# Layer 0's down product by one level of Strassen's scheme, in a fused two-layer diffusion backbone on one core

## The reference

```python
D_FF = (8 * D_MODEL // 3) // 128 * 128        # 2688 = 21 chunks of 128
def conv_ffn(h, w_up, conv_w, conv_b, w_down):
    u = h @ w_up
    ...                                        # convolution over tokens, per channel
    a, b = jnp.split(u, 2, axis=-1)
    return (jax.nn.gelu(a) * b) @ w_down       # (768 x 2688) @ (2688 x 1024) in layer 0
def post_add(x, y, g, gate):
    return x + gate * rms_norm(y, g)           # follows it; y is the product
```

## Time and profile before

| | |
|---|---|
| median of 3 runs | 1529.39 us (1529.23 to 1532.17) |
| profiled execution, first to last instruction | 1530.5 us; no other time is recorded for it |
| instructions | 21741 |
| mean granted TensorE clock | 0.985 of full speed |
| busy: TensorE, VectorE, ScalarE, GpSimd | 1458.3, 966.0, 697.7, 585.9 us |

### The profile page before, as it was taken

One profiled execution on the slowest core, in us unless ns is written; L12 is line 12 of the kernel. 1 busy time (PEld: TensorE's weight loads), 2 busy tenths in 40 slices (PEclk: granted clock), 3 DMA queues, 4 the chain that ended last, 5 costly groups with the idle time before them and its releaser, 6 DMA issues.

```text
span 1530.5 us, 21741 instructions
## 1 busy us (share of the span) xinstructions
PE 1458.3 (95%) x7604; PEld 1192.9 (78%) x7604; DVE 966.0 (63%) x1463; ACT 697.7 (46%) x1184; POOL 585.9 (38%) x516
## 2 busy tenths in 40 slices
PE   4989899999999999999999899899999999999998
PEld 1877567778888888887888688677778888888886
DVE  2368787568678667833346578798876544446445
ACT  3323676444333233223354445588774544444222
POOL 2331545333322222223335522475543444444443
PEclk8999999999999999999999899899999999999999
DMA  8230840223455345411122122010003233333331
GB/s 352 62 97 3 303 175 19 84 97 116 128 156 170 112 126 170 123 63 55 57 70 79 55 75 74 28 42 1 1 9 89 84 97 97 97 98 112 99 97 72
DMA packets 126154, 147.06 MB, mean 96 GB/s; under 512 B 6964, under 2 KB 95288, under 8 KB 125056
## 3 DMA queue, kind: packets, MB, share of 16 engines
q1 hardware_dynamic: 125440, 145.81, 30.1%
q10 hardware_dynamic: 640, 0.26, 0.1%
HBM read 143.92 MB, written 2.14 MB: 95 GB/s over the span
## 4 chain that ended last, share of the span: by engine, by line
PE 86%; DVE 5%; ACT 3%; DMA 2%; issue 2%; POOL 1%; SPq 0%; POOLq 0%; DVEq 0%; ACTq 0%
PE ps L515 24%; PE ps L516 24%; PE ps L517 23%; PE ps L1522 4%; PE ps L1508 4%; PE ps L1533 2%; PE ps L1535 2%; DMA start_w<-in_ada_w_dram 2%; PE ps L1416 1%; PE ps L1010 1%; ACT prob L1564 1%; PE ps L882 1%; DMA ada_w<-in_ada_w_dram 1%; POOL prob L1694 0%; ACT pT_hi L1579 0%
## 5 line engine op out<-in xcount | busy, mean ns | idle before, releaser
L507 POOL TENSOR_TENSOR w_lo<-raw,w_hi 128x1024 fp32r<-128x1024 f32 (+1 forms) x158 | 335.1, 2124 | 586.9 <-ACT w_hi L501 586.9
L515 PE MATMUL ps<-hT_hi,w_hi 128*128 128x512 f32 (+1 forms) x1096 | 387.4, 354 | 4.4 <-DVE hT_lo L1988 3.7
L516 PE MATMUL ps<-hT_lo,w_hi 128*128 128x512 f32 (+1 forms) x1096 | 385.0, 351 | 0.0
L517 PE MATMUL ps<-hT_hi,w_lo 128*128 128x512 f32 (+1 forms) x1096 | 382.7, 349 | 0.0
L501 ACT ACTIVATE w_hi<-raw 128x1024 fp32r<-128x1024 f32 (+1 forms) x179 | 168.8, 944 | 182.6 <-PE ps L517 159.8
L515 PEld LDWEIGHTS ps<-hT_hi,w_hi 128*128 128x128 f32 x1096 | 207.3, 189 | 41.6 <-DVE hT_lo L1988 5.6
L517 PEld LDWEIGHTS ps<-hT_hi,w_lo 128*128 128x128 f32 x1096 | 206.5, 188 | 28.8
L516 PEld LDWEIGHTS ps<-hT_lo,w_hi 128*128 128x128 f32 x1096 | 207.2, 189 | 26.6
L2448 DVE TENSOR_TENSOR g_lo<-act_g,g_hi 128x768 fp32r<-128x768 f32 (+1 forms) x55 | 86.1, 1571 | 126.2 <-ACT g_hi L2398 125.9
L515 PE MATMUL ps<-w_hi,g_hi 128*128 128x512 f32 x380 | 148.2, 390 | 0.8 <-DVE g_lo L2448 0.5
L517 PE MATMUL ps<-w_hi,g_lo 128*128 128x512 f32 x380 | 148.0, 390 | 0.0
(11 more groups left out here) (267 smaller groups left out, 2458.1 us busy)
## 6 DMA issues: line engine op xcount, KB each, us to landing
raw<-in_ffn_w_up_dram SPq DMA_DIRECT2D x84, 512.0 KB, 3.9
ada_w_up<-in_ada_w_dram SPq DMA_DIRECT2D x48, 512.0 KB, 4.2
ada_w<-in_ada_w_dram SPq DMA_DIRECT2D x32, 512.0 KB, 4.8
raw<-in_ffn_w_down_dram SPq DMA_DIRECT2D x42, 256.0 KB, 2.6
raw<-in_ffn_w_down_dram SPq DMA_DIRECT2D x21, 512.0 KB, 3.5
start_w<-in_ada_w_dram SPq DMA_DIRECT2D x8, 1024.0 KB, 8.5
raw<-in_c_w_qkv_dram SPq DMA_DIRECT2D x12, 512.0 KB, 3.7
raw<-in_ab_w_in_dram SPq DMA_DIRECT2D x8, 512.0 KB, 4.1
```

The source lines that it names most:

```text
L507: by.tensor_tensor(split_to(w_lo, phase, m, width), split_from(phase, m, width), split_to(w_hi, phase, m, width).bitcast(F32), ALU.subtrac ...
L515: nc.tensor.matmul(outp, s_hi, m_hi, start=first, stop=False, skip_group_check=True)
L516: nc.tensor.matmul(outp, s_hi, m_lo, start=False, stop=False, skip_group_check=True)
L517: return nc.tensor.matmul(outp, s_lo, m_hi, start=False, stop=last, skip_group_check=True)
```

## The change

The down product of layer 0 is done by one level of Strassen's scheme. Tokens are cut in two halves of 384 (three tiles), the output columns in two of 512, and the first 20 contraction chunks in two of 10; the 21st chunk is added to four of the products as units of its own. Seven products of ten chunk pairs and four odd units make 74 units, each of three tiles, nine matmuls of 512 columns. A unit's left operand is an activation chunk of 384 tokens or the sum or difference of two, its right operand a weight block of 512 columns or the sum or difference of two.

- Weights: the queue loads one or two blocks of 128 x 512 into a ring of five slots (`fast_load`); VectorE adds or subtracts them in place (`fast_w_sum`, 52 of the 74 units); ScalarE rounds (`fast_w_hi`); GpSimd takes the remainder (`fast_w_lo`). The rings of both parts are six deep.
- Activations: VectorE sums two blocks of 384 columns (`fast_g_sum`, 50 units), ScalarE rounds, VectorE takes the remainder (`fast_g_lo`, all units).
- Between products, results in PSUM are copied out (ScalarE) or combined with what is in `yf` in SBUF (VectorE). The first three tiles are finished within the loop, the last three in a tail of six units tile by tile.
- The first six `w_lo` and the first two activation splits are made in the last turn of the up stage. `ada1_small_loads` stands between the loads of units 9 and 10. Some semaphores of both layers are merged into one with offsets.

The order of the products and the units that follow is 5, 1, 3, 4, 7, 2, 6:

```diff
-UNITS = {..., "down0": 2 * FT, ...}
+UNITS = {..., "down0": 0, ...}
...
+PRODUCTS = {
+    1: (((0, 0), (1, 1), 1), ((0, 0), (1, 1), 1)),
+    2: (((1, 0), (1, 1), 1), ((0, 0), None, 0)),
+    3: (((0, 0), None, 0), ((0, 1), (1, 1), -1)),
+    4: (((1, 1), None, 0), ((1, 0), (0, 0), -1)),
+    5: (((0, 0), (0, 1), 1), ((1, 1), None, 0)),
+    6: (((1, 0), (0, 0), -1), ((0, 0), (0, 1), 1)),
+    7: (((0, 1), (1, 1), -1), ((1, 0), (1, 1), 1)),
+}
+PRODUCT_ORDER = ((5, (0, (1,))), (1, None), (3, None), (4, None), (7, (0, (0, 1))), (2, (1, (0,))), (6, (1, (0, 1))))
...
+FAST_TAIL = 6
+FAST_RAW, FAST_W, FAST_G = 5, 6, 6
...
+        def fast_load(sp, u):
+            if u < RAW:
+                sp.wait_ge(lo_split, FIRST_UNIT["proj1"] - RAW + u + 1)
+            elif u == RAW:
+                sp.wait_ge(s("ada_sum"), 8)
+            if u >= FAST_RAW:
+                sp.wait_ge(s("fast_lo"), u - FAST_RAW + 1)
...
+        def fast_sync(sp):
+            for u in range(len(FAST)):
+                if u == 2 * FAST_RAW:
                     after_phase(sp, 5)
                     ada1_small_loads(sp)
+                fast_load(sp, u)
+
+        def fast_w_sum(dve, u):
+            if FAST_SUMS[u]:
+                fast_landed(dve, u)
...
+                    nc.vector.tensor_tensor(first, first, second, ALU.add if sign > 0 else ALU.subtract
+                                            ).then_inc(s("fast_sum"), 1)
+
+        def fast_w_hi(act, u):
...
+            if u >= FAST_W:
+                act.wait_ge(used["down0"], u - FAST_W + 1)
+            nc.scalar.activation(fast_w(w_hi, u), fast_raw[u % FAST_RAW][:, 0:BANK], ACT.Copy).then_inc(s("fast_hi"), 1)
+
+        def fast_w_lo(pool, u):
+            pool.wait_ge(s("fast_hi"), u + 1)
+            nc.gpsimd.tensor_tensor(fast_w(w_lo, u), fast_raw[u % FAST_RAW][:, 0:BANK], fast_w(w_hi, u).bitcast(F32),
+                                    ALU.subtract).then_inc(s("fast_lo"), 1)
...
+        def fast_tensor(pe):
...
+            for u in range(tail):
+                product = FAST[u][0]
+                ready(u)
+                for i in range(HALF_T):
+                    if product != before:
+                        bank_free(product, i)
+                    mm = unit(u, i, product != before and FAST_FIRST[product], False)
+                mm.then_inc(used["down0"], 1)
...
+            for i in range(HALF_T):
+                for u in range(tail, len(FAST)):
+                    if i == 0:
+                        ready(u)
+                    mm = unit(u, i, False, u == len(FAST) - 1)
...
+        def fast_scalar(act):
+            for i in range(2, len(FAST)):
+                fast_g_hi(act, i)
+                if FAST_W <= i + 3 < len(FAST):
+                    fast_w_hi(act, i + 3)
...
+        def fast_vector(dve):
...
+            for i in range(2, len(FAST)):
+                if i + 3 >= FAST_RAW and i + 3 < len(FAST):
+                    fast_w_sum(dve, i + 3)
+                if i + 1 < len(FAST):
+                    fast_g_sum(dve, i + 1)
+                fast_g_lo(dve, i)
+                if i == FAST_END[3] - 4:
+                    dve.wait_ge(s("gates_out"), 16)
+                    ada1_bias(dve)
+                if i == FAST_END[3] + FAST_AFTER + 2:
+                    ada1_columns(dve)
+                for t in range(HALF_T):
...
+                    if i == end[7] + 3 + t:
...
+                        nc.vector.tensor_tensor(yf[:, t, :], yf[:, t, :], gate[:, 0, :],
+                                                ALU.mult).then_inc(s("ffnpost0_post"), 1)
...
+            for t in range(HALF_T):
+                fast_gate_early(dve, HALF_T + t)
+            x_normed(dve, "mix1", 0)
+            x_normed(dve, "mix1", 2)
+            for t in range(HALF_T, ALL_T):
...
+                nc.vector.tensor_tensor(fast_second(t), fast_acc(6, t - HALF_T), fast_second(t),
+                                        ALU.add).then_inc(s("fast_c"), 1)
```

More of the change, by code:

```diff
@@ L63, with fast_units, chunk @@
 BIAS_ROWS = 2 * 2 * FT
+HALF_T = ALL_T // 2
+HTOK = HALF_T * P
+PAIRS = FT // 2
+PRODUCTS = {
[7 rows of a table added]
+}
+PRODUCT_ORDER = ((5, (0, (1,))), (1, None), (3, None), (4, None), (7, (0, (0, 1))), (2, (1, (0,))), (6, (1, (0, 1))))
+def fast_units():
+    units, ends = [], {}
+    for product, odd in PRODUCT_ORDER:
+        g, w = PRODUCTS[product]
+        for k in reversed(range(PAIRS)) if product == PRODUCT_ORDER[-1][0] else range(PAIRS):
+            def chunk(half):
+                return k + PAIRS * half
+            gs = [(chunk(at[1]), at[0]) for at in g[:2] if at]
+            ws = [(chunk(at[0]), at[1]) for at in w[:2] if at]
+            units.append((product, gs, g[2], ws, w[2]))
+        if odd:
+            units.append((product, [(FT - 1, odd[0])], 0, [(FT - 1, c) for c in odd[1]], 1))
+        ends[product] = len(units) - 1
+    return units, ends
+FAST, FAST_END = fast_units()
+FAST_TAIL = 6
+FAST_RAW, FAST_W, FAST_G = 5, 6, 6
 PROJ = {
@@ L1763, in post_root, with post_pool @@
                                     ALU.pow).then_inc(s(f"{tag}_yr"), 1)
-        def post_pool(pool, tag, nt, then):
-            for t in range(nt) if then else ():
+        def post_pool(pool, tag, nt):
+            for t in range(nt):
                 post_epsilon(pool, tag, nt, t)
-            for t in range(nt):
-                if not then:
-                    post_epsilon(pool, tag, nt, t)
                 post_root(pool, tag, nt, t)
[L1772 to L1775, removed]
         def first_halves(nt, t, tag):
@@ L1786, in post_count @@
                 return 4 * t + step + 1
+            if tag == "ffnpost0":
+                return 3 * t + step
             if tag == "mixpost1":
@@ L1815, in post_add @@
                                                op0=ALU.mult, op1=ALU.add).then_inc(s(f"{tag}_post"), 1)
[L1817 to L1824, removed]
-                x_normed(dve, then, nt - 1)
         def out_batches(l, nt):
@@ L2319, in down_sync @@
+        def fast_sync(sp):
+            for u in range(len(FAST)):
+                if u == 2 * FAST_RAW:
                     after_phase(sp, 5)
                     ada1_small_loads(sp)
-                with sp.Fori(0, DTURNS) as i:
-                    for m in range(3):
-                        src = ffn_w_down[l][bass.ds(i * (3 * P) + m * P, P), half * BANK:(half + 1) * BANK]
-                        load_unit(sp, f"down{l}", half * FT + m, src, BANK, i, 3)
-        def down_acc(half, t):
-            return bank(7 if half and t == ALL_T - 1 else t)
```

463 lines of the change are left out of this document (298 added, 165 removed).

## The result

The changed kernel takes 1555.36 us (median of 4 runs, 1553.66 to 1557.81) where the kernel before, beside it, takes 1530.02 (4 runs, 1529.23 to 1532.17): ratio 1.0163, 95% interval 1.0149 to 1.0177. It is slower by 25.3 us; the forecast was 20.9 (1550.3, range 1540 to 1569). The profiled execution is the fastest of the four: it took 1553.66, spans 1551.9 and had a granted clock of 0.985, where the other three had 0.980 to 0.982. For the kernel before the span is 1530.5, also at 0.985.

What follows compares the result with a forecast made beforehand. The prediction took the path shared by VectorE and GpSimd to bound the changed stage: VectorE's loop to 874.9, then the tail, put the last square at 886.6 instead of 865.7, +20.9 us, 1550.3 on the median; range 1540 to 1569.

Steps and rivals of the forecast that it cites:

- The shared path: VectorE operations with two SBUF inputs and GpSimd's exclude each other; one w_lo of 512 columns costs VectorE 1.10 us.
- full steps: Loop steps where VectorE makes both weight and activation sums beside a w_lo: 2.64 us each, 30 steps, against TensorE's 2.08.
- steps with a weight sum alone: Loop steps where VectorE sums weights but no activations: 2.17 us each, 22 steps, 47.7 us.
- PSUM combinations at 0: Nine VectorE combinations reading PSUM escape the lock and lie beside a w_lo otherwise waited for: 0 us, upper bound 5.6.
- The loop as a whole: VectorE's loop from step 2's end at 697.75 to step 73's at 874.9: 161.0 + 15.2 + 1.0 us.
- the start: Stage start: act_g waits for a second GpSimd remainder; step 2 ends at 697.75 and TensorE stands for 2.3 us.
- VectorE's other work: Combinations, gatings, additions to x and ada1 operations in VectorE's loop: 15.2 us.
- Loads: Weight loads hidden except behind the 16 small ada loads, near units 10 and 11: 1.0 us, bounds 0 and 3.
- Tail: Behind the last g_lo TensorE has 39 matmuls, 9.0 us; VectorE's chain ends later, with the last square at 886.6.
- The clock rival: TensorE's pauses in the 30 full steps lower its clock to 1.2 GHz: +37 us, about 1587; chance 0.04.
- The faster one: w_lo does not hold VectorE up, so matmuls decide: 1511 us on the median; chance 0.05.
- The loads rival: Loads set the pace at 3.0 us a unit in products 1 and 7, with a longer stall: 1560; chance 0.06.

Runs made afterwards that it cites:

- e1: The changed kernel with every GpSimd weight remainder w_lo cut from 512 to 8 columns: 1518.36 us, ratio to the kernel before 0.9922.
- e2: The changed kernel, complete, with w_lo made by VectorE behind its g_lo from unit 6 on, not by GpSimd: 1529.55 us, ratio to the kernel before 0.9994.
- e5: The changed kernel with VectorE's 52 weight sums cut to 8 columns, GpSimd left as it is: 1532.0 us, ratio to the kernel before 1.0002.
- e6: The changed kernel, complete, with the 16 small ada loads issued two behind each load of units 10 to 17: 1552.57 us, ratio to the kernel before 1.0147.
- e3: The changed kernel without the product of w_lo with the activations, six matmuls a unit instead of nine: 1553.57 us, ratio to the kernel before 1.0143.
- e4: The changed kernel loading one weight block per unit and summing it with itself, 19 MB instead of 33: 1553.03 us, ratio to the kernel before 1.0146.
- e9: The changed kernel with w_lo on VectorE from unit 6, small loads spread and weight sums cut to 8 columns: 1522.45 us, ratio to the kernel before 0.9949.
- e7: The changed kernel, complete, with w_lo on VectorE from unit 6 and the small loads spread (e2 and e6 together): 1528.04 us, ratio to the kernel before 0.9986.
- e10: As e7, with one addition moved behind VectorE's loop and two normalisations moved into the tail's waits: 1527.98 us, ratio to the kernel before 0.9981.

## Why the prediction was right, point by point

**The shared path.** Right, and to the hundredth: full steps of 2.64 (721.98 - 719.34, and 724.62 behind it), and the steps with a weight sum alone take 4.34 for two (744.76, 749.10, 753.44), so 2.17 each. The changed kernel, every second step of product 3:

```profile
744.76 1.77 DVE L2431 TENSOR_TENSOR raw<-raw 128x512 f32<-128x512 f32 x1
746.45 0.55 DVE L2478 TENSOR_TENSOR fg_lo<-act_g,fg_hi 128x384 fp32r<-128x384 f32 x1
746.92 0.68 DVE L2431 TENSOR_TENSOR raw<-raw 128x512 f32<-128x512 f32 x1
747.64 1.53 DVE L2478 TENSOR_TENSOR fg_lo<-act_g,fg_hi 128x384 fp32r<-128x384 f32 x1
```

e1, e2 and e5 bear out the mechanism from three sides: the w_lo cut away (37.0 us), the w_lo moved to VectorE (25.8 us, 1.10 against 0.60), and the operation behind it cut away (1.09 left). One reading of mine is off by a hundredth: GpSimd's starts in the earlier trace rows are 1.96 apart, not 1.97.

**PSUM combinations at 0.** Right in the mechanism, not in the count. Beside a w_lo of the changed kernel the combination takes its usual 0.60, and the sum behind it is shorter by as much (1.05 instead of 1.65):

```profile
829.73 1.65 DVE L2457 TENSOR_TENSOR fg_sum<-act_g 128x384 f32<-128x384 f32 x1
...
832.71 0.68 DVE L2654 TENSOR_TENSOR yf<-ps,yf 128x512 f32<-128x512 f32 x1
833.31 1.05 DVE L2457 TENSOR_TENSOR fg_sum<-act_g 128x384 f32<-128x384 f32 x1
```

The Trainium skill's rule ("SBUF — State Buffer", section "SBUF: two separate sides"), that VectorE takes part in the lock only with two SBUF inputs or in a 2-port mode, agrees with these rows, as it did with the earlier trace rows. But only five of the nine lay beside a w_lo (807.77, 810.41, 813.05, 832.71 and 835.86). Those at 759.42 and 837.89 met none and cost 0.60, and those at 761.09 and 763.67 began 0.36 ahead of theirs and saved only 0.19 of the sum behind them (1.59 instead of 1.78). Together that is 2.0 us where I had 0.

**The loop as a whole.** I had step 2 end at 697.75 and the last g_lo at 874.9. They ended at 699.0 and 877.94, 3.0 later. Of this 1.04 is the first matmul (692.37 against 691.33): the stage began later in this execution, and in the profiles of the ten experiments, alike up to there, it began at 690.96 to 693.34. Another 0.2 is in the start itself. The other 1.7 are the difference of larger misses. Added up by steps from VectorE's rows, the 19 full steps 10 to 19 and 40 to 48 took 50.0 us where I had 50.2. VectorE's other work took 17.9 and not 15.2; the combinations above are 2.0 of these 2.7. And steps 3 to 9, with the load stall, took 15.1 and not 16.0. That the sum comes out so close is in part luck.

**Loads.** The place was right. VectorE waited 2.9 us, at my bound of 3, but the stall didn't cost that much: a w_lo that started at 708.23, while VectorE stood, cost it nothing. e6, without the waits, needs 13.9 us for steps 3 to 9, so the stall cost the loop 1.2, close to my 1.0. What I had wrong in these steps is that a w_lo costs 1.10 in each.

**Tail.** One term was mis-sized. I had TensorE end 9.0 us behind the last g_lo, at the pace of the old tail and so ahead of VectorE's chain, which set the end. The changed kernel's TensorE behind its last wait:

```profile
876.54 0.77 PE L558 MATMUL ps<-w_hi,fg_hi 128*128 128x512 f32 x1 [1.01 <-DVE fg_lo L2478]
877.10 0.63 PE L559 MATMUL ps<-w_lo,fg_hi 128*128 128x512 f32 x1
877.53 0.63 PE L560 MATMUL ps<-w_hi,fg_lo 128*128 128x512 f32 x1
...
883.17 0.39 PE L559 MATMUL ps<-w_lo,fg_hi 128*128 128x512 f32 x1
883.40 0.39 PE L560 MATMUL ps<-w_hi,fg_lo 128*128 128x512 f32 x1
```

The first matmuls start 0.43 apart, at 1.2 GHz, and only from 881.3 on 0.23 apart. When the last g_lo was out (877.94), 42 matmuls were still to come and not 39, as TensorE had yet to begin unit 72. The last one ends at 889.25, 11.3 behind the last g_lo, and VectorE, which has waited 0.22 for it, sums the tile:

```profile
889.27 0.69 DVE L2680 TENSOR_TENSOR yf<-ps,yf 128x512 f32<-128x512 f32 x1 [0.22 <-PE ps L560]
890.00 0.69 DVE L2683 TENSOR_TENSOR zf<-yf,gate 128x512 f32<-128x512 f32 x1
```

The square starts with the second of these, at 890.00; forecast 886.6. My chain gave 11.7 from the last g_lo to the square, the chip 12.1. Without VectorE's two waits for TensorE, 0.35 at 885.19 and 0.22 here, it would be 11.5: VectorE's chain was right, and TensorE, 2.3 later than I had it, added 0.6. The clock rival was thus right in kind in one place. The granted clock is 1.00 up to 870, 0.70 over 870 to 872.5 and 0.50 over 872.5 to 880, the stretch where TensorE, in the tail's order, has only three matmuls for a step of VectorE and waits 2.08, 1.89 and 1.01 us between them. In the full steps before, where it would have cost 37 us, the clock was 1.00 (712 to 737, 780 to 870; product 4 has one stretch at 0.92, 758 to 780). That this holds for any pauses of this kind is not shown: e3, with longer ones, has 0.82 to 1.00.

**The sum.** Start 1.04 late, then 197.6 instead of 174.4 us from the first matmul to the last square: the stage ends 24.3 later, 3.4 over the forecast. Behind it the program took 661.9 us instead of 664.8, so the spans differ by 21.4 only; the medians differ by 25.3. That the spans agree so well with 20.9 is luck, these 2.9 us; by the medians the forecast was 4.4 us low.

**Rivals.** The faster one is refuted by the 2.64 and, from the other side, by e1, which takes away the w_lo that it took to be harmless. The clock rival is refuted by the 1.00 in the full steps. The loads rival is refuted by e4, but for its stall.

## What to carry to other kernels

Before work is moved to GpSimd or added on VectorE, count the operations with two SBUF inputs on both in one step of the loop: they are one resource, and what GpSimd does there costs VectorE more (1.10 us for 512 columns) than doing it itself (0.60). A scheme that halves the work per weight block halves the time in which the block must be prepared; compare the preparation with the shorter time and not with today's idle shares. And price the end of such a stage by itself: with the block's preparation nearly free (e9) 8.9 of 20.8 us arrived. The rest went to the start, to the last product, where other work of VectorE and ScalarE had been free, and to a granted clock of 0.83 to 0.92 in three stretches.

## What the runs showed of the hardware that was not expected

**GpSimd can be kept from a 128x1 operation for 16 us.** GpSimd in e2, where VectorE has two-input operations back to back from 821.05 on:

```profile
818.43 0.19 POOL L2595 TENSOR_SCALAR ssum<-ssum 128x1 f32<-128x1 f32 x1 [1.22 <-ACT ps L2554]
...
821.38 15.84 POOL L2595 TENSOR_SCALAR ssum<-ssum 128x1 f32<-128x1 f32 x1 [2.12 <-ACT ps L2554]
837.30 0.55 POOL L2590 TENSOR_TENSOR rms<-ssum,minus_half 128x1 f32<-128x1 f32 x1
```

It ends at 837.22, just when VectorE's last operation is out (836.49 + 0.68 = 837.17), and VectorE had stopped because it needed the very value that follows from it; VectorE goes on at 837.94. The same happens at 841.62 (5.15 us, until VectorE waits for ScalarE at 846.7), and e7 has such a row of 11.66 us at 817.55. With w_lo of 512 columns the engines alternate, and in the changed kernel a 128x1 operation gets its turn within 1.05 us (841.36). Why not here is open. The operation of 0.19 us at 818.43 lies beside one of VectorE that reads PSUM.

**A clock that falls or not, 100 us later.** Where attention begins TensorE is partly idle, busy for only 5 to 7 of 10 us. In the kernel before the granted clock is down there and for 10 us behind it; in the changed kernel, at the same place of its program (104.3 us behind the last square), it isn't. Before, then the changed kernel (windows):

```profile
970.00:980.00 10.00, 6.65 (x28) 4.90 (x28) 5.38 (x10) 5.76 (x10) 2.54 (x2) 0.69 0.00 0
980.00:990.00 10.00, 9.34 (x41) 7.77 (x40) 7.13 (x14) 7.13 (x14) 5.92 (x5) 0.63 0.15 50
```

```profile
994.30:1004.30 10.00, 5.23 (x30) 3.63 (x28) 6.68 (x12) 5.86 (x10) 2.62 (x3) 1.00 0.00 0
1004.30:1014.30 10.00, 8.91 (x52) 6.99 (x52) 8.31 (x16) 8.96 (x18) 7.37 (x7) 1.00 0.30 107
```

From the last square to the end before takes 664.8 us, e5 664.7 and e10 664.8, all three with 0.62 to 0.69 there. The changed kernel takes 661.9, and e1, e2, e4 and e6 to e9 take 661.3 to 661.7, all eight with 1.00; e3 lies between, 662.9 with 0.74 and 0.75. This is the 2.9 us of the sum above, and why e10's profile is longer than e7's though its stage is not. Which of the two an execution gets was not controlled by any run here; with it the difference of two profiles is uncertain by 3 us, and medians of several runs are needed for less.
